# Two-layer trunk with a 32-expert mixture: row lists of expert tiles 0 and 1, and the place of the shared expert's down product

## What is computed

```python
scores = sigmoid(t @ w_router)                 # 384 x 32
# group-limited choice of 4 experts per row, weights w normalised and scaled by 2.5
gu = einsum('nd,edf->nef', t, w_exp_gu)        # 1024 -> 512 per expert
a = silu(gu[..., :256]) * gu[..., 256:]
routed = (a * combine) @ w_exp_down            # 256 -> 1024 per expert
sgu = t @ w_sh_gu
shared = (silu(sgu[:, :256]) * sgu[:, 256:]) @ w_sh_down
x = x + g2 * rms_norm(routed + shared, g_post2)
```

## Time and profile before

| | |
|---|---|
| median of 3 runs | 2116.08 us (2113.89 to 2118.29) |
| the profiled execution | 2117.09 us |
| its span, first to last instruction | 2115.5 us |
| PE busy / DVE / ACT / POOL | 89% / 54% / 42% / 20% |
| mixture of layer 0: head, loop, tail | about 633 to 688, 688 to 1011, 1011 to 1054 us |
| bytes moved by DMA | 419.97 MB, mean 199 GB/s |

### The profile page before, as it was taken

One profiled execution on the slowest core, in us unless ns is written; L12 is line 12 of the kernel. 1 busy time (PEld: TensorE's weight loads), 2 busy tenths in 40 slices (PEclk: granted clock), 3 DMA queues, 4 the chain that ended last, 5 costly groups with the idle time before them and its releaser, 6 DMA issues. The chain is left out here.

```text
span 2115.5 us, 26897 instructions
## 1 busy us (share of the span) xinstructions
PE 1874.5 (89%) x8784; PEld 1322.4 (63%) x8784; DVE 1140.9 (54%) x1670; ACT 886.2 (42%) x1510; POOL 425.4 (20%) x485
## 2 busy tenths in 40 slices
PE   6998998999978999999169989989999779999990
PEld 3886666888764666555038866568887646655550
DVE  2345557444545666665523455575444556666655
ACT  3342346433342555554133423464333525555541
POOL 2003312400004222332120042114000042333320
PEclk9999998999999999999589999989999999999995
DMA  8433271343434899998374423704334349999973
GB/s 297 155 122 114 88 252 27 111 138 120 139 143 148 327 346 344 340 344 293 128 271 143 137 96 118 242 7 130 120 123 156 147 150 326 350 345 341 343 265 155
DMA packets 114892, 419.97 MB, mean 199 GB/s; under 512 B 18992, under 2 KB 26768, under 8 KB 82544
## 3 DMA queue, kind: packets, MB, share of 16 engines
q1 hardware_dynamic: 90368, 372.28, 50.1%
q0 software_dynamic: 20928, 40.06, 6.2%
q10 hardware_dynamic: 3504, 6.43, 0.8%
HBM read 411.77 MB, written 32.18 MB: 210 GB/s over the span
## 5 line engine op out<-in xcount | busy, mean ns | idle before, releaser
L1381 DVE TENSOR_TENSOR W_split<-W,W_split 128x2048 fp32r<-128x2048 f32 (+3 forms) x96 | 224.7, 2343 | 407.5 <-ACT W_split L1022 407.5
L1890 PE MATMUL psum<-W_split,qT_split 128*128 128x512 f32 (+3 forms) x1536 | 405.3, 376 | 8.3 <-ACT hT L991 8.1
L1022 ACT ACTIVATE W_split<-W 128x2048 fp32r<-128x2048 f32 (+3 forms) x96 | 175.9, 1838 | 406.1 <-PE psum L1890 370.5
L1890 PEld LDWEIGHTS psum<-W_split,qT_split 128*128 128x128 f32 x1536 | 284.9, 190 | 57.8 <-ACT hT L991 8.7
L1890 PE MATMUL psum<-W_split,scratch_split 128*128 128x512 f32 x864 | 275.4, 391 | 0.6 <-DVE hT_split L1376 0.6
L1830 PE MATMUL psum<-W,zf 128*96 128x512 f32 (+1 forms) x560 | 257.0, 602 | 14.9 <-ACT zf L1282 11.8
L1779 DVE TENSOR_TENSOR W_split<-W,qT_split 128x2048 fp32r<-128x2048 f32 x64 | 146.7, 2292 | 207.0 <-ACT qT_split L1254 207.0
L1254 ACT ACTIVATE qT_split<-W 128x2048 fp32r<-128x2048 f32 x64 | 122.6, 1916 | 235.1 <-DMA W<-in_w_exp_gu 141.7
L1890 PE MATMUL psum<-W_split,hT_split 128*128 128x512 f32 x576 | 210.1, 392 | 5.8 <-DVE scratch_split L1579 5.8
L2135 PE MATMUL psum<-qT_split,hT_split 128*96 128x512 f32 x512 | 199.5, 451 | 6.3 <-issue 6.3
L2135 PE MATMUL psum<-W_split,hT_split 128*96 128x512 f32 x512 | 203.1, 397 | 0.0
(11 more groups left out here) (317 smaller groups left out, 2652.4 us busy)
## 6 DMA issues: line engine op xcount, KB each, us to landing
W<-in_w_exp_gu SPq DMA_DIRECT2D x128, 1024.0 KB, 10.4
W<-in_w_exp_down SPq DMA_DIRECT2D x64, 1024.0 KB, 9.4
W<-in_w_in SPq DMA_DIRECT2D x60, 1024.0 KB, 5.1
W<-in_w_mod SPq DMA_DIRECT2D x48, 1024.0 KB, 4.9
W<-in_w_br SPq DMA_DIRECT2D x16, 1024.0 KB, 5.1
W<-y_rows SPq DMA_DIRECT2D x6, 2048.0 KB, 13.1
W<-in_w_out SPq DMA_DIRECT2D x8, 1024.0 KB, 5.0
kT<-mod_rows POOLq DMA_DIRECT2D x8, 512.0 KB, 5.3
```

The source lines that it names most:

```text
L1022: nc.scalar.activation(high(j), piece(SPLITS[j]), ACT.Copy).then_inc(S["high_ready"], 1)
L1381: V.tensor_tensor(piece(SPLITS[j], Wr), piece(SPLITS[j]), high(j).bitcast(F32), ALU.subtract).then_inc(S["low_ready"], 1)
L1890: ins = nc.tensor.matmul(bank(job, piece_size(key)[1]), act_part[:, k0 + k, t * P:(t + 1) * P], w_part[:, k, :], start=first and (k, i) == ...
```

## The change

It does four things in the mixture of each layer.

1. **Rows of tiles 0 and 1.** As soon as the counts are there, DVE compares for expert 0 and expert 1, for each block of tokens, the place of each token with the numbers 0 to 95 (a new constant row, `places`) and multiplies by whether the token chose the expert: six operations 128x96 (`first_hot`). PE multiplies these with the token numbers (job `first`, 6 products of one column), between shared blocks 1 and 2, and DVE copies the two columns to `first_index`. POOL fetches the rows of both tiles after 2 of its 12 table writes (`fetch_rows`) instead of after the table came back. A place that no row takes holds 0, so that row 0 is fetched for it. The other 10 writes, the read of the table and the fetches for tiles 2 and 3 follow.
2. **Shared down product.** PE no longer makes it in the head, but after the last step of the loop, into six banks of its own (`BANKS_SHARED`); DVE reads it from PSUM in the first of the four sums of each block, and the sums stand in `ybuf` instead of `acc`. The six copies to `acc` are gone. The down weights get a place of their own in `zf` (`shared_dn`), loaded after expert 1's gate/up weights; down slot 1 holds expert 1's weights from the start.
3. **Order in the head.** ACT and DVE split expert 0's weights before the shared expert's last blocks are done, and DVE makes the first shared product ahead of the slot numbers. The transposes of the shared product come after those of the fetched rows.
4. **Banks.** The jobs of the head have fixed banks.

```diff
-    jobs.add(("gu", "s", 0), "dve")
-    jobs.add(("place",), "act")
-    for t in range(1, T):
-        jobs.add(("gu", "s", t), "dve")
-    for t in range(T):
-        jobs.add(("aT", "s", t), "act")
-        jobs.add(("y", "s", t, 0), "dve")
-        jobs.add(("y", "s", t, 1), "dve")
+    jobs.add(("gu", "s", 0), "dve", 5)
+    jobs.add(("place",), "act", 6)
+    jobs.add(("gu", "s", 1), "dve", 7)
+    jobs.add(("first",), "dve", 3)
+    jobs.add(("gu", "s", 2), "dve", 4)
...
+    for t in range(T):
+        jobs.add(("aT", "s", t), "act", 5 + t)
...
 # SP
-                    load_down(1, rows(a["w_sh_down"], l))
                     load_gate_up(0, expert("w_exp_gu", 0))
                     load_down(0, expert("w_exp_down", 0))
+                    load_down(1, expert("w_exp_down", 1))
 
                     sp.wait_ge(*filled(("gu", "s", T - 1)))
                     load_gate_up(1, expert("w_exp_gu", 1))
-                    sp.wait_ge(*filled(("y", "s", T - 1, 1)))
-                    load_down(1, expert("w_exp_down", 1))
+                    sp.wait_ge(S["x_ready"], T)
+                    sp.dma_start(shared_dn, rows(a["w_sh_down"], l).rearrange("(p k) n -> p k n", p=P)).then_inc(S["shared_dn_landed"], 16)
 # POOL
+                    pool.wait_ge(S["rows_out"], 16 * T)
                     for i in range(T * TOPK):
+                        if i == 2:
+                            pool.wait_ge(*emptied(("first",)))
+                            for e in range(2):
+                                fetch_rows(e, first_index)
...
-                    for e in range(2):
-                        gather(e, e, 1)
 # DVE
+                    product_shared(0)
...
                     link(V.tensor_scalar(pos, counts[:, 0:T], -1.0, None, ALU.add))
+                    for e in range(2):
+                        for t in range(T):
+                            ins = V.tensor_scalar(first_hot[:, e, t, :], places, pos[:, t, e:e + 1], rt[:, R_RANK, t, e:e + 1],
+                                                  ALU.is_equal, ALU.mult)
+                    ins.then_inc(S["first_hot"], 1)
...
                     V.tensor_copy(slot_u, slot_f).then_inc(S["slots_ready"], 1)
+                    product_shared(1)
+                    empty(("first",), first_index[0:CAP, :], bank(("first",), 2, slice(0, CAP)))
...
+                            if k == 0:
+                                halves = psum[:, BANKS_SHARED[t]:BANKS_SHARED[t] + 2, :]
+                                row = sums[:, t].rearrange("p (c n) -> p c n", c=2)
+                                ins = V.scalar_tensor_tensor(row, row, weight[:, i:i + 1], halves, ALU.mult, ALU.add)
 # PE
+                    shared_gate_up(1)
+                    pe.wait_ge(S["first_hot"], 1)
+                    bank_free(("first",))
+                    for e in range(2):
+                        ins = multiply(psum[0:CAP, J.bank(("first",)), e:e + 1], [(first_hot[:, e, t, :], choice_f[:, t * TOPK, 0:1]) for t in range(T)])
+                    ins.then_inc(S["psum_filled"], 1)
+                    shared_gate_up(2)
...
+                    pe.wait_ge(S["shared_dn_landed"], 16)
+                    for t in range(T):
+                        if t == 2:
+                            pe.wait_ge(*job_emptied(turns - 1, 1, "y1", LESS["dve"][1]))
+                        for c in range(2):
+                            ins = multiply(psum[:, BANKS_SHARED[t] + c, :], [(shared_T[:, t, f, :], shared_dn[:, f, c * C:(c + 1) * C]) for f in range(2)])
+                        ins.then_inc(S["shared_down"], 1)
```

More of the change, by code:

```diff
@@ L79 @@
 RANK_COLS = NE * NE
+PLACES = RANK_COLS // 2
 def constants():
@@ L111, in constants @@
         lam[layer] = [init, 1.0 - init]
-    return k, np.ascontiguousarray(earlier.astype(np.float32)), lam
+    return k, earlier, lam
 class PsumJobs:
```

118 lines of the change are left out of this document (60 added, 58 removed).

## The result

| | before | changed |
|---|---|---|
| median, 5 runs each on one chip | 2116.15 us (2113.89 to 2120.14) | 2105.16 us (2101.89 to 2106.45) |
| ratio to before, 95% interval | | 0.9946, 0.993 to 0.9962 |
| span of the profiled execution | 2115.5 us | 2104.1 us |

What follows compares the result with a forecast made beforehand. The head bounds the start of a fixed-length loop, through POOL's table chain that brings the first rows; 12.0 or 14.0 us gained, 13 taken, in each of two layers makes 26: 2117.1−26=2091.1, predicted 2091, range 2080 to 2105.

Steps and rivals of the forecast that it cites:

- the write ends at 653.1+0.85=653.9: Head, POOL's second table write: held by one DVE low-weight operation on expert 0, until 0.85 us behind its end.
- my first branch: Head, about 650.8: DVE goes before POOL's second write and holds it; tile 0's rows at 659.4, gain 12.0 us a layer.
- the two branches: Head: DVE or POOL first at 650.9; tile 0's rows at 659.4 or 657.4, gain 12.0 or 14.0 us, 13 taken.
- my 665.05: Layer 0, start of PE's first expert product if DVE goes first, against 677.06 before.
- the rows of tile 0 are there 3.3 later, at 659.4: Head: tile 0's fetch ends at 656.1 if DVE goes first, and its rows land 3.3 us after that.
- The rows of tile 1 never decide: Head, PE: tile 1's transposes follow tile 0's by 3.19 us for the banks; its fetch ends only 1.5 after the first.
- My own sign of being wrong: PE, head: wrong if the first expert product starts after 668, or PE waits many microseconds for tile 2's rows.
- the head is what counts, the loop is a block: Each layer: the loop has fixed length, PE busy 79.97 of 80 us, and starts when the head lets it.
- The rival in which nothing changes: Loop, fed by DMA at 0.97: a head gained is given back as waits for weights; about 2115, chance 0.03.
- the table chain as the next bound: Table chain: cover one microsecond, nothing lost; as rival, last write caught by a load, gain 5.5 a layer, 2106, chance 0.15.
- 2 us decide: Table chain: last table write issued at 669.4, next gate/up load at 671.6; if caught, write and read add 4 each.
- My first rival: Head: DVE does not hold POOL and the clock stays at 1.00; 16.3 us a layer, 2084.5, chance 0.20.

Runs made afterwards that it cites:

- The kernels that end the long hold: Five kernels that stop DVE from holding POOL's second table write for 5 us, by reordering DVE's operations or adding DVE waits: 2091.6, 2092.5, 2094.0, 2094.0 and 2095.5 us.
- the kernel with one gap: Changed kernel, with DVE waiting for the end of its first low-weight operation on expert 0 before it issues the second: 2091.6 us (0.9887).
- the kernel with the loads put off: Changed kernel, with SP issuing expert 1's gate/up and the shared down weights only after the rows of tiles 0 and 1 landed: 2107.5 us (0.9943).
- The halves alone: Two kernels: shared down product moved, with the new DVE and ACT order, 2116.25 us (0.9994); early fetch only, on the kernel before, 2117.4 us (0.9998).
- the first experiment: The kernel without the hold: changed kernel, DVE's table operations first, its low weights waiting for POOL's semaphore behind the second fetch: 2095.5 us (0.9889).
- the copy on POOL: Changed kernel, with one small copy on POOL ahead of the second table write, meant to shift that write against DVE's low-weight operations: 2107.3 us (0.9948).

## Why the prediction was wrong

**Wrong: "the write ends at 653.1+0.85=653.9".** That was my first branch, in which DVE holds POOL for the one operation it meets, as the earlier trace rows showed. It was held over three, to 655.97. By this alone the first fetch ended at 657.44 instead of 656.1, 1.3 us late. I had taken the length of the hold from one instance of before and given the two branches 2 us between them; no bound was set above it. The kernels that end the long hold took 2091.6 to 2095.5 us, and 2091.0 was the forecast. That this is so near is in part luck. In layer 0 of the kernel with one gap the first product came at 667.23, 2.2 later than my 665.05, and from it to tile 2's transposes it was 16.4 instead of my 18.1, with a granted clock of 0.99 to 1.00 from 668 on, where I had kept 0.51 and 0.59. The two errors cancel.

**Wrong: "the rows of tile 0 are there 3.3 later, at 659.4".** They came 7.5 us behind the fetch's end. This is the larger term: 4.2 us. I looked up whether a transfer meets a load of weights for the table chain, where I gave 7.1 us, but for the first fetch I took the 3.26 of before, beside which SP issued only one load of 1 MB (669.46, 1.13 behind the fetch's start), and did not set SP's row beside it. SP's load waits for PE's shared block 2, which I had put at 657.4 myself; the fetch ended at 656.1 in my own sum. The two were 1.3 us apart and I did not see it. The 1.3 us of longer hold closed that distance: the load went out 0.76 behind the fetch's start and 0.40 ahead of its end. A landing of 8.6 us took the place of 4.6, as the kernel with the loads put off shows. With the hold cut (fetch 654.38, load 657.95) the rows came 3.46 us behind the fetch's end, and my 3.3 held.

**Wrong: "The rows of tile 1 never decide".** PE waited 2.46 us for them in the changed kernel, whose second fetch landed in 11.1, and 4.00 with one gap. There they came 4.9 behind tile 0's, where I had 3.2. By my own sum the second fetch started at 656.4, 1.0 ahead of the load at 657.4. The size of this term in the changed kernel is 0.8 us a layer.

The sum of layer 0 closes. The fetch is 1.3 late, the landing 4.2; the rows of tile 1 came 4.01 behind tile 0's instead of 3.2, because their landing too was slow, 0.8. Together 6.3, and the first product came at 671.38 instead of 665.05. From it to tile 2's transposes it was 19.15 instead of 18.1, at a clock of 0.52 between 681 and 688, 1.0 more. So 12 in the first branch became 4.6. Layer 1 went the same way, with the same 5.03 and a wait of 7.29. My own sign of being wrong, a first product after 668, came true.

**Right: the head is what counts, the loop is a block.** From tile 2's transposes to the last ones of layer 0 it was 296.77 us before and 298.15 after, PE busy 100.00 of 100 us in the middle. The rival in which nothing changes falls. The halves alone (0.9994 and 0.9998) show that both are needed, as I said from the backward reading of the chain.

**Right: the other small terms.** Slot numbers by the comparisons: six in 1.53 us, for which I took 1.1 with a bound of 1.4, a little above the bound. The index product: 1.10 us for 12 matmuls, 1.5 taken. The shared transposes: 1.49 us for the six at the low clock, 1.2 taken. The down products in the tail: hidden, 7 us to spare. The sum from PSUM: no dearer at all (1.28 us each).

**Half right: the table chain as the next bound.** In the changed kernel it has no part: the read was done at 675.56 and tile 2's rows waited for nobody. The time of 2106 that I gave this rival is close to the measured 2105.2, by chance. But its mechanism is real, and three kernels ran into it, with PE waiting 5.77 to 8.07 us for tile 2's rows in layer 0 at 2107.1, 2107.6 and 2111.9; so did the kernel with the loads put off. Even with one gap PE waits 0.90 us there. Its price I had summed wrongly: rows at 690.2 leave 5.0 us a layer and not 5.5, so 2107. I had written that "2 us decide" there; 1.4 did. My first rival, no hold and full clock at 2084.5, was the nearer one in its first part (PE into the transposes without a wait, as in the first experiment) and wrong in its second: the clock behind fell to 0.50 between 664 and 668 as well, and the time was 2095.5. (Its fetch of tile 2 should stand 0.4 later by the method of the other branch, which makes it 2085.3.)

**Two rules weighed.** I set the Trainium skill, page "SBUF — State Buffer", section "Who interferes with whom", against the trace: it says that a DVE operation with two SBUF inputs did not stall a transfer issued by GpSimd. The measurements decide against it: 1.9 to 3.0 us for one that meets a low part, 0.97 for one that doesn't, 5.0 in the worst place. Its page "DMA: Bandwidth & Descriptors", section "Queues, rings and completion order", has each DMA engine go round its queues packet by packet, by which a small fetch would hardly be slowed by a large load. Here it is slowed from 4.6 to 8.6 us. What costs those 4 us, no run here shows.

**Open.** Why the copy of the indices in front makes the hold three operations long. In all the traces together, 18 indirect DMA instructions were held by a low part that had another operation directly ahead and one directly behind; the kernel before, with a copy of 128x512 from PSUM ahead, is among them. All 18 were held to the low part's own end. The six instructions of POOL that met a low part with the copy of the indices directly ahead and an operation directly behind were all held over three. The copy alone isn't enough: in the kernel without the hold, the table operations follow it directly, and the write took 1.34 us. No kernel was run with another kind of copy there.

## What to carry to other kernels

Where a small transfer heads a chain that PE waits for, put it on one time axis with the large loads of every queue, by your own predicted instants. The landing depends on how far off the load is (here 4.3 us with the load 4.4 behind the fetch's start, 8.0 with 1.2, 10.3 with 0.03), so a distance of a microsecond or two is a term of its own, and an edit that shortens the chain in one place can push it beside a load in the next. When an engine that only issues DMAs shows a duration several times its usual one, look for the other engine's operation that ends just before it does; a wait of 0.1 us on that engine may be the cure. And when two halves of a change are each worth nothing, measure both alone before you explain their sum.

## What the runs showed of the hardware

- POOL is held by DVE's 128x2048 subtraction with two SBUF inputs. In the traces of all fourteen kernels 121 indirect DMA instructions started while one ran. 111 ended 0.83 to 0.90 us behind it, 1.9 to 3.0 us long in place of 0.97; four ran over three operations; six that started 0.02 to 0.03 us into it were not held (0.97). A plain copy on POOL ends some 0.04 behind it.
- With a 0.15 us DVE copy directly ahead, with no gap, the hold ran over three operations: 5.02 to 5.04 us for the table write, 4.49 and 4.50 for the copy on POOL. A gap of 0.03 to 0.04 us between recorded times was enough to end it earlier.
- An early fetch of 96 rows, counted from the start of its instruction, landed in 4.1 to 5.5 us where SP's loads (2 or 3 MB) began 3.0 us or more behind it, in 7.4 to 8.3 where they began 1.2 behind, in 7.8 and 8.6 with 0.76, in 10.1 and 10.3 with 0.03, in 10.1 and 11.1 where the first load was 0.7 ahead, and in 12.2 and 12.6 where it was 1.4 ahead. One load of 1 MB, 1.1 behind the fetch of the kernel before, did nothing to it (4.2).
- A multiply-and-add of 128x1024 takes 1.28 us, with one input in PSUM as with all in SBUF.
